# RWKV head pairs: the triangular inverse as power products to blocks of 8 and doublings to 64, in place of power products to 16 and a product over the blocks

## What is computed

```python
def step(S, inp):
    r_t, w_t, k_t, v_t, a_t, b_t = inp
    sa = jnp.einsum('bhij,bhj->bhi', S, a_t)
    S = S * w_t[:, :, None, :] + sa[..., None] * b_t[:, :, None, :] + v_t[..., None] * k_t[:, :, None, :]
    y = jnp.einsum('bhij,bhj->bhi', S, r_t)
    return S, y
```

## Time and profile before

| | |
|---|---|
| median of 3 runs | 1220.34 us (1217.95 to 1220.59) |
| profiled execution, its time | 1218.87 us |
| its span in the trace | 1217.1 us |
| TensorE matmul busy | 1144.6 us, 94% of the span |
| VectorE busy | 529.2 us, 43% |
| ScalarE busy | 425.1 us, 35% |
| GpSimd busy | 205.6 us, 17% |

### The profile page before, as it was taken

The page is one execution under the profiler, slowest core; times in us unless marked ns, Lnnn a source line. Parts: engine busy times, 40 slices in busy tenths (PEclk is TensorE's granted clock), DMA queues, the critical chain, the costliest instruction groups (busy, mean ns, idle before and its releaser), DMA issues.

```text
span 1217.1 us, 29462 instructions
## 1 busy us (share of the span) xinstructions
PE 1144.6 (94%) x12520; PEld 627.2 (52%) x12520; DVE 529.2 (43%) x1004; ACT 425.1 (35%) x823; POOL 205.6 (17%) x234
## 2 busy tenths in 40 slices
PE   6999999999999989999998889999999999998785
PEld 5365555555555644555554445544554555554442
DVE  6756464664555510511111125899941511111125
ACT  5345354454454421321121124555443321111123
POOL 2000000000000000222222110688800112221110
PEclk9999999999999999999999999999999999999998
DMA  4017311011011258799999998126702889999996
GB/s 162 3 55 297 116 56 41 20 59 42 20 59 49 98 201 339 283 354 421 423 420 423 424 379 344 70 71 253 316 1 75 324 304 422 422 423 422 422 401 256
DMA packets 53779, 281.97 MB, mean 232 GB/s; under 512 B 14956, under 2 KB 17132, under 8 KB 36496
## 3 DMA queue, kind: packets, MB, share of 16 engines
q1 hardware_dynamic: 43952, 263.73, 54.1%
q0 software_dynamic: 9408, 16.32, 3.7%
q10 hardware_dynamic: 288, 0.03, 0.0%
HBM read 265.84 MB, written 30.41 MB: 243 GB/s over the span
## 4 chain that ended last, share of the span: by engine, by line
PE 79%; DMA 12%; DVE 3%; ACT 2%; issue 2%; SPq 1%; DVEq 0%; ACTq 0%
PE psum L1609 15%; PE psum L974 14%; PE psum L2143 9%; PE psum L2441 8%; PE psum L1790 6%; PE psum L987 6%; DMA h<-rows 5%; DMA big<-in_moe_w_gate_up_dram 4%; DMA h<-in_moe_w_gate_up_dram 4%; PE psum L941 2%; PE psum L1914 1%; PE psum L1779 1%; SPq L423 1%; PE psum L2451 1%; PE psum L2417 1%
## 5 line engine op out<-in xcount | busy, mean ns | idle before, releaser
L974 PE MATMUL psum<-big 128*64 128x256 f32 x1536 | 188.4, 388 | 24.0 <-issue 13.2
L1609 PE MATMUL psum<-big 128*128 128x512 f32 x384 | 192.8, 623 | 1.4 <-ACT big L1660 0.2
L974 PEld LDWEIGHTS psum<-big 128*64 128x64 f32 x1536 | 107.0, 138 | 92.2 <-issue 33.1
L1108 DVE SCALAR_TENSOR_TENSOR big<-psum,big 128x128 f32<-128x128 f32 x64 | 22.4, 351 | 292.2 <-ACT big L1058 292.2
L987 PE MATMUL psum<-big 128*64 128x512 f32 x512 | 121.0, 593 | 1.1 <-DMA big<-in_moe_w_down_dram 0.8
L2143 PE MATMUL psum<-big 128*128 128x512 f32 x256 | 115.6, 604 | 0.8 <-ACT big L2544 0.8
L894 POOL DMA_INDIRECT chosen<-big x60 | 59.9, 998 | 312.3 <-ACT big L1069 150.7
L1983 ACT COPY big<-psum 128x512 f32<-128x512 f32 (+1 forms) x112 | 69.1, 649 | 109.8 <-PE psum L1790 107.4
L2386 POOL TENSOR_TENSOR big<-big 128x512 f32<-128x512 f32 x76 | 96.7, 1272 | 36.0 <-ACT big L2526 25.5
L1790 PEld LDWEIGHTS psum<-big 64*64 64x64 f32 x4096 | 71.5, 134 | 49.3 <-issue 48.5
L2441 PE MATMUL psum<-big,conv_w 128*128 128x512 f32 x224 | 96.5, 592 | 0.0
(11 more groups left out here) (290 smaller groups left out, 1395.2 us busy)
## 6 DMA issues: line engine op xcount, KB each, us to landing
big<-in_moe_w_gate_up_dram SPq DMA_DIRECT2D x40, 2048.0 KB, 31.1
big<-in_moe_w_down_dram SPq DMA_DIRECT2D x64, 1024.0 KB, 27.7
conv_w<-in_moe_w_gate_up_dram SPq DMA_DIRECT2D x8, 2048.0 KB, 31.6
h<-in_moe_w_gate_up_dram SPq DMA_DIRECT2D x8, 2048.0 KB, 26.6
big<-in_moe_w_gate_up_dram SPq DMA_DIRECT2D x16, 1024.0 KB, 12.3
big<-in_rwkv_w_rkv_dram SPq DMA_DIRECT2D x24, 512.0 KB, 4.2
chosen<-h SPq DMA_DIRECT2D x8, 1024.0 KB, 12.6
conv_w<-in_conv_w_pw_dram SPq DMA_DIRECT2D x8, 1024.0 KB, 4.8
```

The costliest lines, as they stand in the source:

```text
L974: last = nc.tensor.matmul(o[half * SLOTS:(half + 1) * SLOTS, 0:F_EXP].rearrange("p (u f) -> p u f", u=2), m.xT[e // 2 % 2][:, c, (e % 2) * ...
L1609: last = nc.tensor.matmul(bank[b], m.w[:, n, c, :], x[:, c, :], start=(c == 0), stop=(c == C - 1))
```

## The change

Blocks are inverted by power products up to 8 instead of 16, and then doubled three times (8 to 16, 16 to 32, 32 to 64). Each doubling is a product P of the outside part with the finished early columns of the inverse D, masked and put into a zeroed matrix, and then products of P with D and with D's transpose, which are added to both. These products have 32 columns instead of 64. The transposed inverse of the second head is kept in a second tile, `dt_moved`, on the other half of the partitions, since adds and copies on VectorE move it. At the end D's transpose is applied once to the right-hand sides (`wz`), by two crossings of 64 columns. `dr`, `mm`, `mt`, `m2`, `x1` are gone. That makes 9 crossings with 64 columns and 8 with 32.

TensorE, within a pair (`pe_prepare_k(m, pe, nq, a, b)` is the k matmuls a to b-1 of the next pair):

```diff
-                pe_prepare_k(m, pe, nq, 0, 4)
+                pe_prepare_k(m, pe, nq, 0, 3)
...
-                pe_prepare_k(m, pe, nq, 4, C)
+                pe_prepare_k(m, pe, nq, 3, 5)
...
             wait(m.l2_ready, m.u2_ready)
-            crossing(mat(m.l2), mat(m.u2), 4, 0, CH, 1)
             crossing(mat(m.u2), mat(m.l2), 4, 256, CH, 1).then_inc(m.l4_ps.now(), 1)
...
-                pe_prepare_r(m, pe, nq, 0, 2)
+                pe_prepare_k(m, pe, nq, 5, 7)
...
+            wait(m.l4_plus, m.v2_ready, m.lv_ready)
+            crossing(swapped(m.v2), swapped(m.l4p), 2, 256, CH, 0).then_inc(m.d_ps.now(), 1)
+            crossing(swapped(m.l4p), swapped(m.v2), 4, 0, CH, 0).then_inc(m.dt_ps.now(), 1)
             if more:
+                pe_prepare_k(m, pe, nq, 7, C)
+                pe_prepare_r(m, pe, nq, 0, 1)
...
+            wait(m.d_ready)
+            crossing(mat(m.uo), columns(mat(m.d), 0, 8), 2, 0, CH // 2, 1).then_inc(m.p16_ps.now(), 1)
+            if more:
+                pe_prepare_r(m, pe, nq, 1, 3)
+            wait(m.p16_ready, m.dt_moved_ready)
+            crossing(moved_dt, columns(swapped(m.p16), 0, 8), 6, 0, CH // 2, 0).then_inc(m.d16_ps.now(), 1)
+            crossing(swapped(m.p16), columns(moved_dt, 1, 8), 4, 0, CH // 2, 0).then_inc(m.dt16_ps.now(), 1)
...
+            wait(m.dt64_ready)
+            crossing(moved_dt, swapped_tok(m.att), 6, 0, 2 * CH, 0)
+            crossing(moved_dt, swapped(m.lv), 6, CH, 2 * CH, 0).then_inc(m.wz_ps.now(), 1)
+            if more:
+                pe_prepare_v(m, pe, nq, 1, 2)
             wait(m.wz0_ready, m.wz1_ready)
...
-            if more:
-                pe_prepare_v(m, pe, nq, 1, 2)
```

VectorE and ScalarE, within a pair:

```diff
             TTn(m.ud, four(two_banks(4, 0, 256)), mask(m.u_in), ALU.mult)
-            TTn(m.ld, lb, mask(m.l_in), ALU.mult)
-            TTn(m.lo_, lb, mask(m.l_out), ALU.mult).then_inc(m.masked_l.now(), 1)
+            TTn(m.ld, four(two_banks(4, 256, 256)), mask(m.l_in), ALU.mult)
+            TTn(m.uo[:, 0], bank[4][:, 0:256].rearrange("p (c t) -> p c t", t=CH), outside, ALU.mult)
+            for par in range(2):
+                last = TTn(m.uo[half(par), 1], bank[5][half(1 - par), 0:256].rearrange("p (c t) -> p c t", t=CH),
+                           outside[half(1 - par)], ALU.mult)
+            last.then_inc(m.masked_l.now(), 1)
...
+            evict_product(m.p16_ps, m.p16, 2, 0, 8, near, m.p16_ready, 1)
+            add_columns(m.d16_ps, m.d, 0, 6, 8, m.d_ready, m.d16_ready)
+            add_columns(m.dt16_ps, m.dt, 1, 4, 8, m.dt_ready, m.dt16_ready)
+            move_columns(m.dt16_ready, 8, m.dt16_moved_ready)
...
-            take(m.dr_ps, flat(m.dr), psum[:, 6 * 512:8 * 512], m.dr_ready)
-            take(m.x1_ps, flat(m.x1), psum[:, 4 * 512:6 * 512], m.x1_ready)
```

GpSimd gets ten more mask steps at the start and three memsets in each pair, which VectorE's `evict_product` waits for. At the opening the norm product moves into the r projection:

```diff
+        def pool_rwkv(m, pool):
+            for q in range(PAIRS):
+                pool.wait_ge(m.dt_ps.sem, m.dt_ps.by(q))
+                for x in (m.p16, m.p32, m.p64):
+                    nc.gpsimd.memset(x.rearrange("p h c t -> p (h c t)"), 0.0).then_inc(m.cleared, 1)
...
                 pe_prepare_r(m, pe, 0, c, c + 1)
-            pe_prepare_norm(m, pe, 0)
+                if c == C // 2:
+                    pe_prepare_norm(m, pe, 0)
```

More of the change, by code:

```diff
@@ L1335, in pool_rwkv_masks @@
                 step(sel(out=m.tmp_mask[p, :], in_=one, compare_op=ALU.is_ge, fill=0.0, base=0,
[L1336 to L1339 removed]
+                         pattern=[[-8, CH // 8], [0, 8]], channel_multiplier=1))
@@ new lines, in dve_rwkv_pair, with blocks, half_columns @@
+            for par in range(2):
+                last = nc.vector.tensor_copy(m.dt_moved[half(1 - par)],
+                                             bank[5][half(par), 0:256].rearrange("p (c t) -> p c t", t=CH))
+            last.then_inc(m.dt_moved_ready.now(), 1)
+            def blocks(x, late, block):
+                return x.rearrange("p h c (b x n) -> p h (c b) x n", x=2, n=block)[:, :, :, late]
+            def half_columns(i, lo_, block):
+                return two_banks(i, lo_, 128).rearrange("p h (c n) -> p h c n", n=block)
@@ new lines, in move_columns @@
+            def move_columns(ready, block, done):
+                w(ready)
+                for par in range(2):
+                    to, source = (x.rearrange("p c (b x n) -> p (c b) x n", x=2, n=block)[:, :, 1] for x in (
+                        m.dt_moved[half(1 - par)], m.dt[half(par), 1]))
+                    last = nc.vector.tensor_copy(to, source)
+                last.then_inc(done.now(), 1)
+            near, mid = (x.rearrange("p (c n) -> p c n", n=n) for x, n in ((m.l_near, 8), (m.l_mid, 16)))
@@ L2108, in dve_rwkv_pair @@
[L2108 to L2115 removed]
+            evict_product(m.p32_ps, m.p32, 2, 0, 16, mid, m.p32_ready, 2)
@@ L2118, in dve_rwkv_pair @@
+            for par in range(2):
+                second = m.dt_moved[half(1 - par), :, 32:64]
+                last = TTn(second, bank[5][half(par), 0:128].rearrange("p (c n) -> p c n", n=32), second, ALU.add)
+            last.then_inc(m.dt64_ready.now(), 1)
             w(m.wz_ps)
```

164 lines of the change are left out of this document (91 added, 73 removed).

## The result

| | before | changed |
|---|---|---|
| median | 1219.93 us (1217.95 to 1220.59, 4 runs) | 1232.13 us (1229.95 to 1236.65, 4 runs) |
| ratio to before, 95% interval | | 1.0109 (1.0089 to 1.0128) |
| profiled execution, its span | 1218.87, 1217.1 us | 1236.65, 1234.9 us |

The change costs 12.2 us, 1.1%, by the medians, where I had forecast 8.5. The profiled execution of the changed kernel is the slowest of its four, 4.5 us over its median, and that of before is 1.1 us under its own, so the two traces differ by 17.8 us.

What follows compares the result with a forecast made beforehand. TensorE's own stream was taken to bound the pairs. Terms 5.5 + 0.5 + 0.1 + 1.8 + 0.6 = 8.5 us on the profiled 1218.87 made 1227.4, plus 1.5 for the median, 1228.8; own range 1225 to 1232, 8-in-10 range 1219 to 1234.

Steps and rivals of the forecast that it cites:

- The price of the narrow product: TensorE crossings in the pairs: 32 moving columns cost 0.467 us, as 64 do, because the 64-column weight load fills each round.
- The rivals with cheap products: Crossings in the pairs: 0.26 us each gives 1216.1 us, chance 0.12; half the saving gives about 1222.5, chance 0.08.
- VectorE's stream becomes a wait: Middle pairs: VectorE gets 0.69 us more work, so TensorE idles 1.03 us, first ahead of `v2`, then ahead of `d`.
- Pairs 2 to 6: Middle pairs: 0.1 us of TensorE's stream plus 1.0 of waiting, 1.1 us each, 5.5 us together.
- The later steps are covered: Doublings from p16 to dt64: projections cover the vector operations and GpSimd memsets, costed at nothing.
- The rival in which this cover fails: Doublings in the pairs: strided vector operations or the memset cost more, giving 1233 to 1235 us; chance 0.15.
- Pair 0: First pair: without moment_out, 2.2 us less on VectorE, it waits only for `l2p`; +0.5 us.
- Pair 1: Second pair: its pauses of 1.31 and 2.48 us stay and let VectorE get ahead; +0.1 us.
- Last pair: Thin filling: 14.85 us instead of 12.90 from `d` to the products at L1900; +1.8 us with the earlier start.
- Opening: Before the pairs: the norm product (0.62 us) delays r and ScalarE's r copy and exponentials; +0.6 us.
- The pauses move: Rival: pair 1's pauses and the slow clock after them fall away, giving 1224 us; chance 0.10.

Runs made afterwards that it cites:

- e5: Changed kernel plus four crossings per pair with 32 weight columns, two with 32 moving columns and two with 64; 1246.54 us in a single run.
- e2: Changed kernel with the next pair's cumulated decays moved behind the `v2` copy on VectorE; 1224.34 us, ratio to before 1.0048.
- e3: Changed kernel with one 128x512 mask operation for the outside part instead of three of 256 columns, altering part of the computation; 1228.38 us, ratio 1.0072.
- e6: Kernel before with the cumulated decays moved behind the `v2` copy; 1219.9 us, ratio 1.0007.
- e8: Changed kernel with decays behind the `v2` copy and pair 1's stores and load spread over the pairs; 1223.65 us, ratio 1.0036.
- e4: Changed kernel with the eight 1 MB stores and 2 MB load ahead of pair 1 spread over the pairs; 1231.08 us, ratio 1.0104.
- e12: e8's kernel with all eight 1 MB stores issued behind the output projection's weights; 1227.76 us, ratio 1.0065.
- e7: Kernel before with the eight 1 MB stores and 2 MB load spread over the pairs; 1214.98 us, ratio 0.9965.
- e11: e7's kernel with two of pair 5's three stores placed elsewhere, so no two go out together; 1217.2 us, ratio 0.9988.
- e9: Kernel before with decays behind the `v2` copy and the stores and load spread over the pairs; 1216.68 us, ratio 0.9982.
- e10: e8's kernel with two of pair 5's three stores placed elsewhere, so no two go out together; 1225.38 us, ratio 1.0046.
- e1: Changed kernel plus sixteen crossings per pair ahead of p16, with 64, 32 or 16 moving columns or 32-column weights; 1350.6 us in a single run.

## Why the prediction was right, and where its terms were off

**The sign and the size.** The forecast of 1228.8 stands 3.3 us under the measured 1232.13, which lies just past the upper end of its own range (1225 to 1232) and inside the whole one (1219 to 1234). The two mechanisms that it rests on, no saving in a narrow product and a wait for VectorE's written order, are the ones that the runs show; the terms beside them were too small.

**The price of the narrow product** was right: 0.467 us was taken, and 8 x 58.5 ns = 0.468 is measured. The argument, that the load of 64 weight columns fills a round by itself, is shown by the table of e5. The rivals with cheap products are out.

**VectorE's stream becomes a wait** was right in mechanism, and the size came out near by two errors that offset each other. I had 1.03 us ahead of `v2` and `d` in sum; the rows show 0.91, all of it ahead of `v2`, and 1.0 at most. Timeline of the kernel before, the operation that makes `l2p` there:

```profile
223.13 0.68 DVE L2097 TENSOR_TENSOR big<-big 128x512 f32<-128x512 f32 x1
```

By my terms it would end at 223.81 + 0.69 = 224.50, TensorE would be there at 217.21 + 2.78 + 1.56 + 1.92 + 0.47 = 223.94, and with 0.14 to wake the wait ahead of `v2` is 0.70, with the other 0.33 ahead of `d`. To wake took 0.45, not 0.14, since two more semaphores are named behind the late one. That, with small differences in the two streams, moved all of the wait ahead of `v2` and left none ahead of `d`. e2 shows that the order carries the wait, e3 that the added mask operations are 3.8 us of it, e6 that the kernel before didn't need a better order. Pairs 2 to 6 cost 4.83 us together where I had 5.5. Four of them have the wait, 3.6 us; pair 6 has a late instruction packet in its place.

**The later steps are covered** was right: in pairs 0 to 6 no wait for the masking or adding of the doublings shows, and the memsets took 0.52 us each as in the earlier trace rows. The rival in which this cover fails did not come.

**The terms that were mis-sized.** *Pair 0*: 1.26 us against 0.5. I had let the missing `dve_moment_out` make VectorE earlier, but it stands behind `l2p`, and it is `l2p` that TensorE waits for. Timeline of the changed kernel, pair 0:

```profile
78.12 1.16 PE L1810 MATMUL psum<-big 64*64 64x64 f32 x64 [1.00 <-DVE big L2129]
```

*Pair 1*: 1.85 us against 0.1. Both pauses stayed, as forecast, but the first is 2.77 us instead of 1.31 and the second 2.80 instead of 2.48. Chain of the changed kernel, beside the earlier trace rows:

```profile
121.61 2.77 issue
...
129.38 2.80 issue
```

*Last pair*: I had 14.85 us from `d` to the products at L1900 and +1.8 in all. In e2 and e8 it is 15.15 (422.45 to 437.60, 418.24 to 433.39), and the whole last pair 2.35 us longer than before; so the term was 0.55 short. Some 0.2 of it lies ahead of `d` (15.25 us after the pair's start in e2, where I had 15.05) and 0.3 behind it. The trace of the changed kernel itself has +4.8. Timeline of the changed kernel, last pair, beside the earlier trace rows:

```profile
421.65 1.16 PE L1810 MATMUL psum<-big 64*64 64x64 f32 x64 [0.69 <-DVE big L2112]
...
428.96 1.16 PE L1810 MATMUL psum<-big 64*64 64x64 f32 x64
...
432.28 0.32 PE L1810 MATMUL psum<-big 64*64 64x32 f32 x8 [0.62 <-issue]
433.38 1.90 PE L1810 MATMUL psum<-big 64*64 64x32 f32 x64 [0.78 <-DVE big L2158]
...
446.50 0.62 PE L1935 MATMUL psum<-big 64*64 64x64 f32 x26 [1.05 <-DVE big L2196]
```

The pair lost 0.62 us here and 0.87 at 418.42 to late instruction packets, and up to 1.7 to a stretch at 1.2 GHz from 433.5 to 436.9 (the crossings at 433.38 take 1.90 us instead of 1.14). Together that is up to 3.2 us, where the pair is only 2.45 longer than in e2; so a part seems to have fallen into waits that are there anyway. e2 and e8 have none of the stretch.

*Opening*: from the first matmul of the k projection to pair 0 it takes 23.73 us (40.45 to 64.18) against 22.95 (38.07 to 61.02), so +0.8 against 0.6. The other 2.4 us of the late start are not the change's. Most of them come from eight matmuls at L1541. They took 3.75 us in this execution where the same eight took 1.97 in that of before; in the profile of e6, which opens like the kernel before, they took 3.66.

*Missing from the sum*: after the pairs TensorE runs a stretch at 1.2 GHz in both kernels. Windows of the changed kernel and of before, right after the last pair (the last three numbers are clock, transfer share, GB/s):

```profile
456.00:466.00 10.00, 7.98 (x48) 4.09 (x49) 2.14 (x3) 5.32 (x9) 0.00 (x0) 0.66 0.77 326
```

```profile
440.00:450.00 10.00, 7.58 (x52) 3.85 (x50) 2.14 (x3) 5.64 (x10) 0.00 (x0) 0.83 0.79 336
```

A clock of 0.66 over 10 us is 6.8 us at half rate, 0.83 is 3.4; the difference costs 1.7 us. The longer stretch comes with e2, e3, e4, e8 and e12, but also with e7 and e11, which have the old algorithm, and not with e6, e9 and e10; so it is not bound to the change. Nor can one trace of each kernel say how often each of them has it.

**The sum again, with the sizes measured**: opening 0.8, pair 0 1.3, pair 1 1.85, pairs 2 to 6 4.8, last pair 2.35, clock 1.7: 12.8, against 12.2 by the medians. The 4.3 us between it and my 8.5 are pair 1's pauses (1.75), the clock (1.7), pair 0 (0.8), the last pair (0.55) and the opening (0.2), less 0.7 in the middle pairs. The two largest of them are differences between two single executions, and the agreement of 12.8 with 12.2 is no proof of them.

**The pauses move** was a rival with 0.10, and in the measured kernel they stayed. I took them for something that VectorE's progress or the stream's shape could make fall away. They are late instruction packets, and moving the stores takes them out of pair 1 (e4, e7 to e12). Their number and length also differ where the stores stand still: 1.31 and 2.48 us before, 1.32 and 1.38 in e6, 3.05 and 0.62 in e3, 2.77, 1.32 and 1.17 in e2. One profile of each kernel can't tell whether that is the code or the execution.

## What to carry to other kernels

Halving one side of a small matmul saves nothing while the other side is still 64 wide: look at the weight's columns before paying for more steps and more change-overs. When a change shortens the producer's stream between two dependent steps, walk the order of the other engine up to the operand that is needed first, and move what nobody waits for behind it; here that was worth 7.8 of 12.2 us by the medians, 5.9 of them seen in the pairs. When an engine waits for several semaphores, look which one comes last: here each name behind it took another 0.15 us. A pause without a releaser on TensorE is worth a look at the instruction queue: large stores beside dense small products cost more than they seem. Moving them gave the fastest version, e7 (1214.98 us, ratio 0.9965); its near relatives e9 and e11 kept 0.2% and 0.1% of the 0.35%.

## What the runs showed of the hardware

- The packets of 16 KB on the instruction queue go through the same transfer engines as the data, and TensorE goes on 1.2 to 1.6 us after a late one has landed. That they carry its instructions is read from this and from e12. Starts of packets were never closer than 3.3 us, so crossings of 64 records in 0.47 us can't go on for long: in e1 they mostly ran 2 to 3 us between pauses of 1.0 to 1.7.
- Packets were late behind a single 1 MB store: e10's pauses began 5.2 us after a store was issued (211.08 and 216.31, 344.90 and 350.16), with one or two loads of 512 KB in flight. Other stores of the same kernel drew none, and in e12 those loads without stores drew none over 0.71 us.
- During or after a pause the granted clock often fell to 1.2 GHz, for 3.4 or 6.8 us and in e1 for up to 10.2 in the pairs; after e11's pause of 1.63 us it didn't. There a round of four took 106.5 to 107 ns with 64 weight columns, at 32 and at 16 moving columns alike, and 53.5 with 32 weight columns: the weight load goes with the clock.
- A wait on TensorE costs by the names behind the late semaphore: from the end of VectorE's operation to the start of TensorE's next matmul it was 0.15 us with one name, 0.30 with two and 0.45 with three, in every such wait of the pairs, within 0.01.
